# Two transformer blocks on one core: three late sums of squares as pairs of fp32r matmuls, and the last four residuals ahead of the low parts

## The chip, the core and the metric

The kernel runs on one core of one Trainium2 chip. The metric is the device time of one execution in microseconds. The program runs five engines that wait for each other through semaphores: TensorE (matmuls, written PE in the profile), VectorE (DVE), ScalarE (ACT), GpSimd (POOL) and SyncE (SP), which issues the loads of weights.

## The reference

Two blocks run one after the other on 512 positions of width 1024 (the first with 16 meta tokens in front). The first has a sparse attention with chosen keys, a short convolution, a gated mix and a feed forward part; the second has a linear recurrence, two kinds of attention and a feed forward part with a convolution. What matters here are the norms:

```python
def rmsnorm(x, g):
    xf = x.astype(jnp.float32)
    y = xf * lax.rsqrt(jnp.mean(xf * xf, axis=-1, keepdims=True) + EPS)
    return (y * g.astype(jnp.float32)).astype(x.dtype)

# first block, after the mix
h = h + mixed @ w_out[i]
f = rmsnorm(h, norm_ffn_g[i])                      # "ffn"
h = h + (silu(f @ w_gate[i]) * (f @ w_up[i])) @ w_down[i]
out = rmsnorm(h, norm_final_g)                     # folded with the next into "n1"
# second block
h = rmsnorm_2(x, norm1_g[l]); proj = h @ w_in[l]
...
x = x + mixed @ w_out[l]
h2 = rmsnorm_2(x, norm2_g[l])                      # "n2"
u = causal_dwconv(h2 @ w_ff_up[l], conv_ff_w[l], conv_ff_b[l])
...
return rmsnorm_2(x, final_g)                       # "fin2"
```

All inputs and outputs are float32.

## The kernel before

**Layout.** The residual H lies transposed in SBUF, as 8 chunks of 128 channels by 512 positions. Weights come in panels of 1024x128. SyncE loads a panel into RAW (4 slots, a slot is loaded again when its panel has been used), and GpSimd splits it: WH is the value rounded to fp32r (L584), WL the rest (L586), both with SBUF inputs. Operands are split in the same way: ScalarE writes the high part (AH or BH), VectorE the low part (AL or BL). A panel is then 8 chunks of three fp32r matmuls of 512 columns: WH with high, WL with high, WH with low (L645).

**Norms.** The scale 1/rms is applied late, behind the matmuls, since it is the same for all channels of a position. So the panels behind a norm start from the gained but unscaled residual, while the sum of squares is still being made. ScalarE squares each chunk of H, VectorE adds the squares chunk by chunk into SS (128 partitions), and TensorE adds up the partitions in `late_sum` (L714 to L717) and `between_sums` (L908 to L912) by a float32 matmul of `ones` with SS, put between panels that it can do meanwhile. ScalarE takes the root (L1332, L1358), VectorE the reciprocal (L1789, L1841), and the products in PSUM are scaled by it. The norm n1 needs two sums, SS and SSB, since it stands for two norms in a row. The norm fin2 is done in another way and has nothing to do with this change.

**Where the sums stand on TensorE.** For ffn, after 7 of the 8 chunks of two panels. For n1, after the first two panels of stage xa. For n2, after panels 0 and 1 (chunk by chunk in turn, L673 to L675) and half of panel 2 of the stage gv0.

**The end of the second block's output projection.** The stage wo2b has two panels, each holding two chunks of four output rows (`last_rows`, L1044). It writes to four PSUM banks in turn: the first panel gives rows 0 to 3, the second rows 4 to 7, and row 4 + b can start only when VectorE has added row b to H (`last_residual`, L2040 to L2045, which counts up `wo2_free`). Behind each residual ScalarE makes BH and the square (L1491, L1492), and VectorE makes BL (L2051):

```python
for o in range(2):
    last_residual(o)
for o in range(KC):
    dve.wait_ge(b_hi, B_USE["n2"] + o + 1)
    stt(out=BL[:, o], in0=H[:, o], ...)
    for r in ((2, 3, 4), (5,), (6,), (7,))[o] if o < 4 else ():
        last_residual(r)
```

Then come seven additions of squares (L2059), each waiting for the one before, the last of which writes SS. The order of the work on each engine is the order in which the code is written.

Of the kernel before, what the change touches and what calls it, by code (L numbers as in the profile page):

```python
# [15 lines left out]
F32 = mybir.dt.float32  # L16
# [6 lines left out]
P = 128  # L23
# [93 lines left out]
def two_blocks(nc, x, meta_tokens, norm_mix_g, w_in, w_attn_out, conv_w, w_conv_out, w_out, norm_ffn_g, w_gate,  # L117
# [3 lines left out]
    with ExitStack() as ctx:  # L121
        def sem(name):
            return ctx.enter_context(nc.semaphore(name))
# [16 lines left out]
        def again(reg, start):  # L140
            return [start, reg[1]]
# [54 lines left out]
        rq2 = again(r_q, q0)  # L196
        XA = place(rq2, "XA", [P, 4, T + 3])
        YA = place(rq2, "YA", [P, 4, T])
        L = [place(again(r_q, q0), "L0", [P, 2, 2, T]), place(again(r_b, b0 + 4 * 8 * T), "L1", [P, 2, 2, T])]

        rq3 = again(r_q, q0)
# [58 lines left out]
        T2 = place(rt4, "T2", [P, 2, T])  # L260
        rt9 = again(r_t, t0)
        SQB = place(rt9, "SQB", [P, 2, T])
        SSB = place(rt9, "SSB", [P, T])
        SQ8 = place(again(r_t, t0), "SQ8", [P, KC, T])
        SQT = place(rt4, "SQT", [P, 2, T])
        SS = place(rt4, "SS", [P, T])
        ROOT = place(rt4, "ROOT", [P, T])
        rt5 = again(r_t, t0)
# [78 lines left out]
        rstd_ready = {n: sem(f"rstd_ready_{n}") for n in NORMS}  # L347
        LATE = ["ffn", "n1", "n2", "fin2"]
        ss_added = {n: sem(f"ss_added_{n}") for n in LATE}
        ss_summed = {n: sem(f"ss_summed_{n}") for n in LATE}  # L350
        fin_ms = sem("fin_ms")
        gate_scaled, silu_ready, taps_done = sem("gate_scaled"), sem("silu_ready"), sem("taps_done")
# [258 lines left out]
        def _(pe):  # L611
# [101 lines left out]

            def late_sum(name):  # L714

                pe.wait_ge(ss_added[name], KC + 2)
                mm(PX[:, 0, 0:T], ones[:], SS[:], start=True, stop=True).then_inc(ss_summed[name], 1)  # L717

            a_wide = (XH[:, :, 0:N], XL[:, :, 0:N])
            a_x = (XH[:, :, META:N], XL[:, :, META:N])  # L720
# [186 lines left out]

            def between_sums():  # L908

                pe.wait_ge(ss_added["n1"], KC + 2)  # L910
                mm(PX[:, 0, 0:T], ones[:], SS[:], start=True, stop=True)
                mm(PX[:, 1, 0:T], ones[:], SSB[:], start=True, stop=True).then_inc(ss_summed["n1"], 1)  # L912

            stage("xa", b_t, n1, late=1, then=between_sums)
            pe.wait_ge(small_loaded, 16 * (6 + 4))
# [207 lines left out]
        def _(act):  # L1123
# [204 lines left out]
                        go(SQT[:, j], pick(H, c), ACT.Square).then_inc(sq_ready[norm_name], 1)  # L1328

            def root(name):  # L1330
                act.wait_ge(ss_summed[name], 1)
                go(ROOT[:], PX[:, 0, 0:T], ACT.Sqrt, bias=eps_t[:], scale=1.0 / D).then_inc(rt_ready[name], 1)  # L1332

# [13 lines left out]
            with act.Fori(0, KC // 2) as i:  # L1347
                for j in range(2):
                    c = i * 2 + j
                    act.wait_ge(freed["dve"], c + (LETGO["dn2"]["dve"] + 1))  # L1350
                    act.sem_inc(act_seen, 1)
                    go(pick(BH, c), pick(H, c), ACT.Identity, bias=zero_t[:], scale=GF1[:, bass.ds(c, 1)]).then_inc(b_hi, 1)
                    act.wait_ge(ss_added["n1"], c + 1)
                    act.sem_inc(act_seen, 1)
                    go(SQT[:, j], pick(H, c), ACT.Square)
                    go(SQB[:, j], pick(H, c), ACT.Square, scale=VEC[:, 0, bass.ds(c + V_FIN, 1)]).then_inc(sq_ready["n1"], 1)
            act.wait_ge(fin_ms, 1)
            go(ROOT[:], R[:], ACT.Sqrt, bias=eps2_t[:], scale=1.0 / D).then_inc(rt_ready["n1"], 1)  # L1358
            go(RF[:], PX[:, 0, 0:T], ACT.Sqrt, bias=eps_t[:], scale=1.0 / D).then_inc(rt_ready["n1"], 1)
# [164 lines left out]
        def _(dve):  # L1524
# [213 lines left out]
                tt(BL[:, k], QT[:, k], BH[:, k].bitcast(F32), ALU.subtract).then_inc(b_lo, 1)  # L1738
            dve.wait_ge(b_lo, B_USE["y"] + KC)
            nc.vector.memset(WR[:], 0.0).then_inc(wr_cleared, 1)  # L1740
            step(nc.vector.memset(XA[:, :, 0:3], 0.0))


# [31 lines left out]
            def residual(name, scale, to=None):  # L1775
# [3 lines left out]
                with dve.Fori(0, COUNT[name] // 4) as i:  # L1779
                    for j in range(4):  # L1780
# [3 lines left out]
                        if to:  # L1784
                            feed(to[0], i * 4 + j, j % 2, *to[1:])

            def late_scale(name):
                dve.wait_ge(rt_ready[name], 1)
                nc.vector.reciprocal(R[:], ROOT[:]).then_inc(rstd_ready[name], 1)  # L1789
                dve.wait_ge(rstd_ready[name], 1)  # L1790
# [42 lines left out]
                tt(PB6 if c < KC - 1 else SS[:], PB6, SQT[:, c % 2], ALU.add).then_inc(ss_added["n1"], 1)  # L1833


            dve.wait_ge(ss_summed["n1"], 1)
            step(ts(R[:], PX[:, 0, 0:T], EPS, None, ALU.mult))
            settled()
# [181 lines left out]
            step(nc.vector.memset(SBL[:, :, 0:P].bitcast(F32), 0.0))  # L2020
            step(ts(TRI[:, 0], tri[:], 1.0, None, ALU.mult))
            step(ts(TRI[:, 1], nones[:], 1.0, None, ALU.mult))
            for c in range(2):
                sb_mask(2 * c)
                sb_mask(2 * c + 1)
                for i in range(4 * c, 4 * c + 4):
                    rescale(i)
                settled()
                mixed_rows(4 * c)
                mixed_rows(4 * c + 1)  # L2030
                sb_softplus(2 * c)
                sb_softplus(2 * c + 1)
                sb_low(2 * c)
                sb_low(2 * c + 1)
                mixed_rows(4 * c + 2)
                sb_lo(2 * c)
                sb_lo(2 * c + 1)
                mixed_rows(4 * c + 3)
# [5 lines left out]
                    dve.wait_ge(wo2_out, 3 * (o // 4) + o % 4 + 1)  # L2044
                tt(H[:, o], WO2_BANKS[o % 4], H[:, o], ALU.add).then_inc(wo2_free if o < 6 else freed["dve"], 1)  # L2045

            for o in range(2):
                last_residual(o)
            for o in range(KC):
                dve.wait_ge(b_hi, B_USE["n2"] + o + 1)  # L2050
                stt(out=BL[:, o], in0=H[:, o], scalar=VEC[:, 0, V_N2 + o:V_N2 + o + 1], in1=BH[:, o].bitcast(F32),  # L2051
                    op0=ALU.mult, op1=ALU.subtract).then_inc(b_lo, 1)
                for r in ((2, 3, 4), (5,), (6,), (7,))[o] if o < 4 else ():
                    last_residual(r)
            dve.sem_inc(ss_added["n2"], 3)
            for o in range(1, KC):
                dve.wait_ge(sq_ready["n2"], o + 1)
# [81 lines left out]
```

## Time and profile before

| what | value |
|---|---|
| median of 3 runs | 1553.34 us (1552.59 to 1553.67) |
| profiled execution | 1555.63 us |
| its span, first to last instruction | 1553.9 us |
| TensorE busy | 1539.9 us, 99% |
| VectorE, ScalarE, GpSimd busy | 747.5, 395.1, 905.7 us |
| granted TensorE clock, mean | 0.999 of full speed |

The profile is of one execution. "Busy" counts the time in which an engine has an instruction running. The chain of work that ended last is followed back from the last instruction, at each step to what released it. A timeline row has the start in microseconds, the duration, the engine, the line, and what is written from what; in brackets stands how long the engine was idle before it, and what ended that. Matmuls overlap: a row of 0.39 us may stand 0.23 us behind the one before.

### The profile page before, as it was taken

The page shows a single profiled execution, that of the slowest core. Times are in us where ns is not written, and L with a number is a line of the kernel's source. Part 1 is how long each engine was busy: PE and PEld are TensorE (multiplying, and loading weights), DVE is VectorE, ACT ScalarE, POOL GpSimd, SP SyncE. Part 2 cuts the span into 40 slices and gives each one's busy share as a digit, 9 for nine tenths or more (in the row PEclk, how much of TensorE's full clock was granted, in tenths as well). Part 3 has the DMA queues.
Part 4 walks back from the last instruction along what each step waited for, and adds up shares of the span by engine and source line. Part 5 has one row for each costly group of instructions (what it writes and reads, how often), then busy time and mean ns, then how long its engine had stood idle before and what let it go on. Part 6 is the DMA issues. An engine that isn't in the chain of part 4 may idle for free.

```text
span 1553.9 us, 22779 instructions
## 1 busy us (share of the span) xinstructions
PE 1539.9 (99%) x7847; PEld 1291.7 (83%) x7847; DVE 747.5 (48%) x1157; ACT 395.1 (25%) x757; POOL 905.7 (58%) x536
## 2 busy tenths in 40 slices
PE   8999999999999999999999999999999999999998
PEld 7779999988888888888888888777877888888887
DVE  4157840232335354742343245868567751552456
ACT  4221210233442012210010013456564320220122
POOL 5645556544445667766666666653454666666653
PEclk9999999999999999999999999999999999999999
DMA  6223333322223432333333333322222323333322
GB/s 213 82 72 91 85 93 91 86 68 59 64 68 104 147 95 82 108 94 95 100 100 98 95 88 102 93 70 64 60 67 82 94 81 108 96 98 103 95 81 95
DMA packets 266712, 142.67 MB, mean 92 GB/s; under 512 B 6445, under 2 KB 263749, under 8 KB 266389
## 3 DMA queue, kind: packets, MB, share of 16 engines
q1 hardware_dynamic: 265285, 139.16, 30.5%
q10 hardware_dynamic: 1360, 2.56, 0.4%
q8 instruction: 48, 0.79, 0.2%
q14 instruction: 19, 0.16, 0.0%
HBM read 137.38 MB, written 4.19 MB: 91 GB/s over the span
## 4 chain that ended last, share of the span: by engine, by line
PE 95%; DVE 3%; ACT 1%; issue 1%; DMA 0%; ACTq 0%; DVEq 0%
PE PS L645 74%; PE PS L643 12%; PE PS L872 1%; PE PS L849 1%; PE PS L957 1%; PE PS L797 1%; DVE BL L2051 1%; PE PS L875 0%; PE PS L923 0%; PE PS L848 0%; PE PS L862 0%; DVE L L1881 0%; PE PS L1003 0%; DVE L L1864 0%; ACT SBX L1422 0%
## 5 line engine op out<-in xcount | busy, mean ns | idle before, releaser
L586 POOL TENSOR_TENSOR WL<-RAW,WH 128x1024 fp32r<-128x1024 f32 (+1 forms) x259 | 622.7, 2404 | 21.6
L584 POOL TENSOR_SCALAR WH<-RAW 128x1024 fp32r<-128x1024 f32 (+1 forms) x259 | 280.4, 1083 | 607.6 <-DMA RAW<-in_w_in_dram 257.5
L645 PE MATMUL PS<-BH,WH 128*128 128x512 f32 x928 | 366.6, 395 | 1.2 <-DVE BL L2051 1.1
L645 PE MATMUL PS<-BL,WH 128*128 128x512 f32 x928 | 361.4, 389 | 0.0
L645 PE MATMUL PS<-BH,WL 128*128 128x512 f32 x928 | 361.1, 389 | 0.0
L645 PEld LDWEIGHTS PS<-BH,WH 128*128 128x128 f32 x928 | 174.2, 188 | 42.4 <-issue 4.4
L645 PE MATMUL PS<-AH,WH 128*128 128x512 f32 x528 | 205.9, 390 | 0.0
L645 PE MATMUL PS<-AL,WH 128*128 128x512 f32 x528 | 205.4, 389 | 0.0
L645 PE MATMUL PS<-AH,WL 128*128 128x512 f32 x528 | 205.4, 389 | 0.0
L645 PEld LDWEIGHTS PS<-BH,WL 128*128 128x128 f32 x928 | 174.3, 188 | 37.2 <-issue 1.7
L645 PEld LDWEIGHTS PS<-BL,WH 128*128 128x128 f32 x928 | 174.2, 188 | 36.6
L645 PE MATMUL PS<-XH,WH 128*128 128x512 f32 x288 | 119.9, 416 | 0.0
L645 PEld LDWEIGHTS PS<-AH,WH 128*128 128x128 f32 x528 | 99.1, 188 | 21.2 <-issue 1.0
L645 PEld LDWEIGHTS PS<-AL,WH 128*128 128x128 f32 x528 | 99.1, 188 | 20.6
L645 PEld LDWEIGHTS PS<-AH,WL 128*128 128x128 f32 x528 | 99.1, 188 | 20.3
L645 PE MATMUL PS<-XH,WL 128*128 128x512 f32 x288 | 112.3, 390 | 0.0
L645 PE MATMUL PS<-XL,WH 128*128 128x512 f32 x288 | 112.3, 390 | 0.0
L643 PE MATMUL PS<-XH,WH 128*128 128x264 f32 (+2 forms) x528 | 107.3, 284 | 0.4 <-DVE XL L1583 0.4
L643 PE MATMUL PS<-XH,WL 128*128 128x264 f32 (+2 forms) x528 | 106.5, 283 | 0.0
L643 PE MATMUL PS<-XL,WH 128*128 128x264 f32 (+2 forms) x528 | 106.5, 283 | 0.0
L1783 DVE SCALAR_TENSOR_TENSOR H<-PS,H 128x512 f32 x40 | 27.6, 691 | 141.5 <-PE PS L645 141.5
L643 PEld LDWEIGHTS PS<-XH,WH 128*128 128x128 f32 (+1 forms) x528 | 81.3, 187 | 1.9 <-DVE XL L1583 0.7
(334 smaller groups left out, 1817.4 us busy)
## 6 DMA issues: line engine op xcount, KB each, us to landing
RAW<-in_w_in_dram SPq DMA_DIRECT2D x89, 512.0 KB, 3.4
RAW<-in_w_ff_up_dram SPq DMA_DIRECT2D x44, 512.0 KB, 3.6
RAW<-in_w_gate_dram SPq DMA_DIRECT2D x22, 512.0 KB, 3.6
RAW<-in_w_up_dram SPq DMA_DIRECT2D x22, 512.0 KB, 3.6
RAW<-in_w_down_dram SPq DMA_DIRECT2D x16, 512.0 KB, 3.6
RAW<-in_w_ff_down_dram SPq DMA_DIRECT2D x16, 512.0 KB, 3.6
RAW<-in_w_out_dram SPq DMA_DIRECT2D x10, 512.0 KB, 3.7
RAW<-in_w_conv_out_dram SPq DMA_DIRECT2D x8, 512.0 KB, 3.7
```

What stands on the lines that cost most here:

```text
L584: nc.gpsimd.tensor_scalar(WH[:, slot, 0:kc], RAW[:, slot, 0:kc], 1.0, 1.0, ALU.mult, ALU.mult).then_inc(w_hi, 1)
L586: nc.gpsimd.tensor_tensor(WL[:, slot, 0:kc], RAW[:, slot, 0:kc], WH[:, slot, 0:kc].bitcast(F32), ALU.subtract).then_inc(w_ready, 1)
L643: last = mm(into[0:rows, h, 0:wide], w[:, w_at, k, 0:rows], a[:, k, h * wide:(h + 1) * wide], start=st, stop=sp_)
L645: last = mm(bank_of(name, i)[0:rows], w[:, w_at, k, 0:rows], a[:, k, :], start=st, stop=sp_)
L797: last = mm(dst[:, 0:min(EXT[b], BANK)], lhs, KI[r:r + 64, 0:min(EXT[b], BANK)], start=True, stop=True)
L849: mm(PX[:, 0, 0:min(large_e, BANK)], QS[:, 1], head[:, 0:min(large_e, BANK)], start=True, stop=True).then_inc(qk_done, 1)
L872: mm(PB7[:, 0 if t <= few else P:2 * P], V[:, t, at], PT[:, 0 if t <= few else 1:2, t * P:(t + 1) * P], start=t == 0, stop=False, skip_gro ...
L957: last = mm(SB_SET[n % 2][:, to - max(SBW[j], 2 * P):to], TRI[:, 0 if j == i else 1], spaced(part, n % 2, j), start=False, stop=True, skip ...
L1783: stt(out=h, in0=bank_of(name, j), scalar=scale, in1=h, op0=ALU.mult, op1=ALU.add).then_inc(freed["dve"], 1)
L2051: stt(out=BL[:, o], in0=H[:, o], scalar=VEC[:, 0, V_N2 + o:V_N2 + o + 1], in1=BH[:, o].bitcast(F32), op0=ALU.mult, op1=ALU.subtract).then_ ...
```

## The change

SS is split like any other operand: ScalarE copies it to SSH, rounded to fp32r, and VectorE subtracts, which gives SSL (in the place of SS). TensorE adds the partitions of both into one PSUM bank with two fp32r matmuls, with ONE, an fp32r copy of `ones`. The same is done with SSB. ONE lies where other tiles come later, so it is written twice. The norm fin2 keeps its matmuls. On VectorE the last residuals are put in another order: four before the first low part, and one behind each of the next four low parts.

```diff
+        rq4 = again(r_q, q0 + 8448)
+        SSH = place(rq4, "SSH", [P, T], F32R)
+        SSBH = place(rq4, "SSBH", [P, T], F32R)
+        ONE = place(rq4, "ONE", [P, P], F32R)
...
+        SSBL = place(again(rt9, rt9[0]), "SSBL", [P, T], F32R)
         SSB = place(rt9, "SSB", [P, T])
...
+        SSL = place(again(rt4, rt4[0]), "SSL", [P, T], F32R)
         SS = place(rt4, "SS", [P, T])
...
+        SUM_USE = {"ffn": 0, "n1": 1, "n2": 3}
...
             def late_sum(name):
-                pe.wait_ge(ss_added[name], KC + 2)
-                mm(PX[:, 0, 0:T], ones[:], SS[:], start=True, stop=True).then_inc(ss_summed[name], 1)
+                pe.wait_ge(one_ready, 2 if name == "n2" else 1)
+                pe.wait_ge(ss_lo, SUM_USE[name] + 1)
+                mm(PX[:, 0, 0:T], ONE[:], SSH[:], start=True, stop=False)
+                mm(PX[:, 0, 0:T], ONE[:], SSL[:], start=False, stop=True).then_inc(ss_summed[name], 1)
...
             def between_sums():
-                pe.wait_ge(ss_added["n1"], KC + 2)
-                mm(PX[:, 0, 0:T], ones[:], SS[:], start=True, stop=True)
-                mm(PX[:, 1, 0:T], ones[:], SSB[:], start=True, stop=True).then_inc(ss_summed["n1"], 1)
+                pe.wait_ge(ss_lo, SUM_USE["n1"] + 2)
+                for n, (own, after_b) in enumerate(((SSH, SSBH), (SSL, SSBL))):
+                    mm(PX[:, 0, 0:T], ONE[:], own[:], start=n == 0, stop=n == 1)
+                    last = mm(PX[:, 1, 0:T], ONE[:], after_b[:], start=n == 0, stop=n == 1)
+                last.then_inc(ss_summed["n1"], 1)
...
             def root(name):
+                act.wait_ge(ss_added[name], KC + 2)
+                go(SSH[:], SS[:], ACT.Copy).then_inc(ss_hi, 1)
                 act.wait_ge(ss_summed[name], 1)
...
+            act.wait_ge(ss_added["n1"], KC + 2)
+            go(SSH[:], SS[:], ACT.Copy).then_inc(ss_hi, 1)
+            go(SSBH[:], SSB[:], ACT.Copy).then_inc(ss_hi, 1)
             act.wait_ge(fin_ms, 1)
...
             nc.vector.memset(WR[:], 0.0).then_inc(wr_cleared, 1)
+            ts(ONE[:], ones[:], 1.0, None, ALU.mult).then_inc(one_ready, 1)
...
+            def sum_low(name, whole, hi, lo, n=1):
+                dve.wait_ge(ss_hi, SUM_USE[name] + n)
+                tt(lo[:], whole[:], hi[:].bitcast(F32), ALU.subtract).then_inc(ss_lo, 1)
+
             def late_scale(name):
+                sum_low(name, SS, SSH, SSL)
                 dve.wait_ge(rt_ready[name], 1)
...
+            sum_low("n1", SS, SSH, SSL)
+            sum_low("n1", SSB, SSBH, SSBL, 2)
             dve.wait_ge(ss_summed["n1"], 1)
...
             step(ts(TRI[:, 1], nones[:], 1.0, None, ALU.mult))
+            ts(ONE[:], ones[:], 1.0, None, ALU.mult).then_inc(one_ready, 1)
...
-            for o in range(2):
+            for o in range(4):
                 last_residual(o)
...
-                for r in ((2, 3, 4), (5,), (6,), (7,))[o] if o < 4 else ():
-                    last_residual(r)
+                if o < 4:
+                    last_residual(o + 4)
```

How it moves the work. On VectorE, from the last residuals to the reciprocal of n2, before (H from PSUM is a residual, BL a low part, SQ the squares):

```order
L2045 TENSOR_TENSOR H<-PS,H 128x512 [waits wo2_out] x2
L2051 SCALAR_TENSOR_TENSOR BL<-H,VEC,BH 128x512 [waits b_hi]
L2045 TENSOR_TENSOR H<-PS,H 128x512 [waits wo2_out]
L2045 TENSOR_TENSOR H<-PS,H 128x512 [waits panel_done]
L2045 TENSOR_TENSOR H<-PS,H 128x512 [waits wo2_out]
L2051 SCALAR_TENSOR_TENSOR BL<-H,VEC,BH 128x512 [waits b_hi]
L2045 TENSOR_TENSOR H<-PS,H 128x512 [waits wo2_out]
```

and now, at the same place and, behind the "...", at the end of the sum:

```order
L2071 TENSOR_TENSOR H<-PS,H 128x512 [waits wo2_out] x3
L2071 TENSOR_TENSOR H<-PS,H 128x512 [waits panel_done]
L2077 SCALAR_TENSOR_TENSOR BL<-H,VEC,BH 128x512 [waits b_hi]
L2071 TENSOR_TENSOR H<-PS,H 128x512 [waits wo2_out]
...
L2085 TENSOR_TENSOR SS<-PS,SQ_128 128x512 [waits ss_added_n2,sq_ready_n2]
L1807 TENSOR_TENSOR SSL<-SS,SSH 128x512 [waits ss_hi]
L1812 RECIPROCAL R<-ROOT 128x512 [waits rt_ready_n2]
```

Residuals 2 and 3 have moved ahead of the first low part, and a subtraction stands between the last addition and the reciprocal.

On TensorE, the sums of n1 between the panels of stage xa, before:

```order
L645 MATMUL PS<-BL,WH 128x512 [waits b_lo]
L911 MATMUL PS<-SS,ones 128x512 [waits ss_added_n1]
L912 MATMUL PS<-SSB,ones 128x512
L645 MATMUL PS<-BH,WH 128x512 [waits b_lo,freed_dve,w_ready]
L645 MATMUL PS<-BH,WL 128x512
```

and now:

```order
L653 MATMUL PS<-BL,WH 128x512 [waits b_lo]
L922 MATMUL PS<-SSH,ONE 128x512 [waits ss_lo]
L923 MATMUL PS<-SSBH,ONE 128x512
L922 MATMUL PS<-SSL,ONE 128x512
L923 MATMUL PS<-SSBL,ONE 128x512
L653 MATMUL PS<-BH,WH 128x512 [waits b_lo,freed_dve,w_ready]
```

Two matmuls have become four, and they wait for the low parts of the sums where they waited for the sums.

## Rows read from the trace of the kernel before

**Rows 1.** The page: busy time of the engines, and the chain by engine.

```profile
PE 1539.9 (99%) x7847; PEld 1291.7 (83%) x7847; DVE 747.5 (48%) x1157; ACT 395.1 (25%) x757; POOL 905.7 (58%) x536
...
PE 95%; DVE 3%; ACT 1%; issue 1%; DMA 0%; ACTq 0%; DVEq 0%
```

**Rows 2.** Chain of waits, around the sum of ffn (start us, us, what).

```profile
599.94 20.40 PE PS L645 x90
620.34 0.86 PE PS L717 x2
```

**Rows 3.** Timeline at the sum of ffn, VectorE and GpSimd (start us, us, engine).

```profile
613.63 0.69 DVE L1773 TENSOR_TENSOR SS<-SS,SQT 128x512 f32<-128x512 f32 x1
614.66 1.04 POOL L584 TENSOR_SCALAR WH<-RAW 128x1024 fp32r<-128x1024 f32 x1 [1.95 <-DMA RAW<-in_w_up_dram]
```

**Rows 4.** Timeline at the sums of n1, VectorE and TensorE.

```profile
979.38 0.68 DVE L1833 TENSOR_TENSOR SS<-PS,SQT 128x512 f32<-128x512 f32 x1
981.51 0.39 PE L645 MATMUL PS<-BL,WH 128*128 128x512 f32 x1
983.69 0.40 PE L645 MATMUL PS<-BH,WL 128*128 128x512 f32 x1
```

**Rows 5.** Timelines: a ScalarE copy, a TensorE restart, GpSimd after n1's sums.

```profile
630.85 0.63 ACT L1345 ACTIVATE AH<-T 128x512 f32 x1 [3.80 <-DVE T L1812]
...
974.80 0.50 PE L645 MATMUL PS<-BH,WH 128*128 128x512 f32 x1
...
985.19 1.05 POOL L584 TENSOR_SCALAR WH<-RAW 128x1024 fp32r<-128x1024 f32 x1 [6.92 <-DMA RAW<-in_w_in_dram]
```

**Rows 6.** Timeline of VectorE from the last residuals to SS of n2.

```profile
1173.03 1.37 DVE L2045 TENSOR_TENSOR H<-PS,H 128x512 f32<-128x512 f32 x2 [2.25 <-PE PS L1049]
1174.61 2.97 DVE L2051 SCALAR_TENSOR_TENSOR BL<-H,VEC,BH 128x512 fp32r<-128x512 f32 x1 [0.21 <-ACT BH L1491]
...
1179.30 1.39 DVE L2051 SCALAR_TENSOR_TENSOR BL<-H,VEC,BH 128x512 fp32r<-128x512 f32 x1
...
1184.04 0.73 DVE L2051 SCALAR_TENSOR_TENSOR BL<-H,VEC,BH 128x512 fp32r<-128x512 f32 x1
...
1185.30 5.51 DVE L2051 SCALAR_TENSOR_TENSOR BL<-H,VEC,BH 128x512 fp32r<-128x512 f32 x4
1190.73 4.71 DVE L2059 TENSOR_TENSOR PS<-PS,SQ 128x512 f32<-128x512 f32 x6
1195.54 0.69 DVE L2059 TENSOR_TENSOR SS<-PS,SQ 128x512 f32<-128x512 f32 x1
```

**Rows 7.** Timeline of GpSimd in the same stretch.

```profile
1174.63 2.40 POOL L586 TENSOR_TENSOR WL<-RAW,WH 128x1024 fp32r<-128x1024 f32 x1
...
1180.23 2.73 POOL L586 TENSOR_TENSOR WL<-RAW,WH 128x1024 fp32r<-128x1024 f32 x1
1185.10 1.06 POOL L584 TENSOR_SCALAR WH<-RAW 128x1024 fp32r<-128x1024 f32 x1 [2.14 <-DMA RAW<-in_w_ff_up_dram]
1186.24 2.69 POOL L586 TENSOR_TENSOR WL<-RAW,WH 128x1024 fp32r<-128x1024 f32 x1
1197.43 1.05 POOL L584 TENSOR_SCALAR WH<-RAW 128x1024 fp32r<-128x1024 f32 x1 [8.49 <-DMA RAW<-in_w_ff_up_dram]
```

**Rows 8.** Timeline of TensorE in the same stretch.

```profile
1174.64 0.39 PE L1049 MATMUL PS<-AH,WL 128*128 128x512 f32 x1
...
1177.36 0.39 PE L1049 MATMUL PS<-AH,WL 128*128 128x512 f32 x1
1178.24 0.50 PE L1049 MATMUL PS<-AH,WH 128*128 128x512 f32 x1 [0.49 <-DVE H L2045]
...
1180.87 0.39 PE L1049 MATMUL PS<-AH,WL 128*128 128x512 f32 x1
...
1192.85 0.39 PE L645 MATMUL PS<-BL,WH 128*128 128x512 f32 x1
...
1197.56 0.39 PE L645 MATMUL PS<-BH,WL 128*128 128x512 f32 x1
```

## What was predicted

> **What bounds the kernel now.** I read the page first: TensorE is busy for 99% of the span, and the chain of work that ended last is 95% TensorE [rows 1]. So time comes off only where TensorE itself does less or waits less; work on another engine counts only where TensorE stands still for it. Then I read the chain of waits around the first late sum, to get two prices. Ninety panel matmuls take 20.40 us there, 0.227 us each, and the f32 matmul over the ones, two records, takes 0.86 us [rows 2]. Last I read the timelines of VectorE, GpSimd and TensorE around each of the three sums [rows 3 to 8]. The reader is to see there when the sum of squares is ready, when TensorE asks for it, and where VectorE is held up behind GpSimd.
>
> **Four f32 matmuls become eight fp32r ones.** The norms ffn and n2 have one sum each, n1 has two: four f32 matmuls at 0.86 us, 3.44 us of TensorE [rows 2]. Each becomes two matmuls of panel kind, 2 x 0.227 = 0.45 us. Saved are 0.41 us each, 1.64 us in all, if nothing waits. As bounds: an fp32r matmul with new operands cannot be below the panel pitch, and if it cost as much as an f32 record (0.43 us) the saving would be nothing. I take the panel pitch, since element kinds and shape are those of a panel matmul. The Trainium skill (FP8 and Floating Point Precision, TensorE Precision Notes) says that true FP32 makes four passes. Four passes at this trace's pitch would be 0.91 us and the saving 1.8 us instead of 1.64; no trace of a pass is visible here, only the two records, so the measured 0.86 stands in the sum.
>
> **What is put in front of each sum.** Before, TensorE needed only SS. Now ScalarE copies SS to SSH (0.63 us, by its copy to AH [rows 5]), VectorE subtracts (0.69 us uncontended, by its addition to SS, also all in SBUF [rows 3]), with some 0.03 us for each hand-over: about 1.4 us from SS to the matmul. ScalarE now loads its square root table behind the copy; there are more than 3 us until the root is wanted at each norm, so that is hidden.
>
> *ffn.* SS is ready at 613.63 + 0.69 = 614.32 [rows 3]. SSH follows at 615.0. The subtraction then meets GpSimd's operation that ends at 615.70 [rows 3] and ends at 616.3. TensorE asks at about 620.2 (the chain row: 599.94 + 20.40 [rows 2]). Slack 3.9 us, so the saving is whole: **-0.41 us**.
>
> *n1.* SS is ready at 979.38 + 0.68 = 980.06 [rows 4]. SSH at 980.72, SSBH half a microsecond later, SSL at 981.43, SSBL at 982.04 (subtractions 0.61 us apart). GpSimd does nothing until 985.19 [rows 5], so none of it is held up. TensorE would ask at 981.51 + 0.23 = 981.74 [rows 4]. It therefore waits to 982.10 and pays 0.11 us at the restart (a first matmul after a wait shows 0.50 us, not 0.39 [rows 5]). Then four matmuls: the second panel matmul behind the sum starts at 982.10 + 0.11 + 5 x 0.227 = 983.35, where it started at 983.69 before [rows 4]. Net **-0.34 us** of the possible 0.82. Behind the waiting matmul on TensorE stand only panels 2 and 3 of xa, which nobody needs early.
>
> *The small copies into ONE* (128x128, twice) stand on VectorE at the start of co and after TRI. I cost them at nothing: in both places VectorE runs on into a wait for TensorE. If that cover were gone, each would be about 0.2 us.
>
> **The reordered residuals (n2).** This is where both edits meet. Before, VectorE does residuals 0 and 1, then the first low part BL, which starts at 1174.61 and lasts 2.97 us [rows 6] because GpSimd's subtraction runs to 1174.63 + 2.40 = 1177.03 [rows 7]; it ends 0.55 us after that. Residual 2 comes behind it, so TensorE, which needs that bank, starts at 1178.24 instead of 1177.36 + 0.23 = 1177.59 [rows 8]: 0.65 us plus 0.11 for the restart, 0.76 us. From 1177.36 to the matmul at 1197.56 [rows 8] there are 12 + 60 + 2 = 74 matmuls and the sum, 74 x 0.227 + 0.86 = 17.64 us; it took 20.20. So 2.56 us were lost: 0.76 for this bank, the rest for low parts that came late.
>
> Now residuals 2 and 3 go ahead. The panel that residual 3 needs ends at 1174.64 + 0.39 = 1175.03 [rows 8], so residual 3 ends at 1175.76. BL 0 starts at 1175.7, inside the same GpSimd operation, and ends at 1177.58 as before: the two residuals are hidden in time that was blocked. The 0.76 us goes. From there every low part comes one place earlier. BL 1 ends at 1178.83. BL 2 ends at 1180.69, where BL 1 ended (1179.30 + 1.39 [rows 6]). BL 3 is held until GpSimd's subtraction is over (1180.23 + 2.73 [rows 7]) and ends at 1183.51, and BL 4 takes the free slot of 0.73 us at 1184.04 [rows 6], to 1184.77. GpSimd's next piece hangs on the last panel of wo2b. That ended at 1180.87 + 0.39 and the piece began 3.84 us later at 1185.10 [rows 7, 8]; now it ends at 1180.47, so the piece begins near 1184.31, in the middle of BL 4, and gets the port behind it. BL 5 then ends near 1186.2, BL 6 is held by the 2.7 us subtraction [rows 7] to 1189.0, BL 7 ends at 1189.65. Before, it ended at 1190.81 (1185.30 + 5.51 [rows 6]).
>
> TensorE starts the gate panels at 1177.59 + 12 x 0.227 = 1180.31 and needs BL k at 1180.31 + 1.36 k. All are in time but BL 6 (1188.47 wanted, 1189.0 there): 0.57 + 0.11 = 0.68 us lost. It would reach the sum at 1180.31 + 60 x 0.227 + 0.68 = 1194.6.
>
> But the sum is not ready. From the end of BL 7 to the end of SS were 1195.54 + 0.69 - 1190.81 = 5.42 us [rows 6], seven dependent additions, unchanged. SS is ready at 1195.07, SSH at 1195.74, and SSL is asked for at 1195.77. At that moment GpSimd is due again: it began 1197.43 - (1192.85 + 0.39) = 4.19 us after the first gate panel ended [rows 7, 8], and that panel now ends near 1191.35. So its conversion (1.05 us) begins near 1195.54 and ends at 1196.59, just ahead of SSL, which has both inputs in SBUF like BL. SSL ends 0.55 us later, at 1197.14. TensorE starts the sum at 1197.18 and the second panel matmul behind it at 1197.18 + 0.11 + 3 x 0.227 = 1197.97, where it started at 1197.56 [rows 8]. Net **+0.41 us**: the stalls of 2.5 us that the new order removes come back as a wait of 2.6 us at the sum.
>
> The Trainium skill (SBUF — State Buffer, SBUF: two separate sides) says that the shared pair of ports goes to whichever of the two engines starts first. Here the row of BL 0 starts 0.02 us ahead of GpSimd's and was held all the same, so the starts in the trace don't settle such close races. For SSL, 0.23 us behind, rule and rows give the same 1197.14; asked for just ahead, the rule gives 1196.5 and the row 1197.14.
>
> **Sum.** -0.41 - 0.34 + 0.41 = -0.34 us. The profiled execution took 1555.63 us, 1.7 us more than its span of 1553.9; it would be 1555.3. The median of the runs shown is 1553.34, 2.3 us less, so I forecast **1553.0 us**, no change. A measurement of this kernel can tell about 0.2%, 3.1 us: faster is below 1550.2, slower above 1556.5.
>
> **Rivals.** *A: SSL gets the port ahead of GpSimd.* If GpSimd is due 0.3 us later or SS is ready 0.3 us earlier, SSL ends at 1196.45, the matmul at 1197.56 is at 1197.3 and n2 gives -0.3: in all -1.0 us, 1552.3. For it: the two are 0.23 us apart and the arrivals of weights in [rows 7, 8] differ by 0.35 us (3.84 and 4.19). Against it: both must shift the right way.
>
> *B, slower: SSL misses the gap between GpSimd's two operations.* If SSL is asked for after 1196.59, the 2.4 us subtraction is under way; SSL ends near 1199.6, TensorE starts 2.5 us later than in the forecast, and the total is -0.34 + 2.5 = +2.1, 1555.5. It decides from 0.8 us more delay on the VectorE chain, or an equal advance of GpSimd. For it: one more held low part is enough. Against: 0.8 us is more than the spread of the arrivals. Were a second low part also held for a whole subtraction, 2 us more, it would pass 1556.5.
>
> *C, faster: the sum keeps up.* If the low parts come free of GpSimd and SSL is there when TensorE asks, the whole is -1.64 - 2.56 = -4.2 us, 1549.1. Against it: seven additions and the new 1.4 us are in series behind BL 7, and TensorE has only 16 matmuls, 3.6 us, between its first use of BL 7 and the sum, where that chain takes 5.4 + 1.4 us.
>
> *D: the fp32r pair is no cheaper than f32* (0.43 us a matmul): -0.34 + 8 x 0.2 = +1.3, 1554.6. Nothing in the rows speaks for it.
>
> **Chances.** Forecast 0.55, A 0.22, B 0.13, C 0.05, D 0.05. Faster by over 0.2% is C, 0.05. Slower by over 0.2% is the worst third of B, 0.04. Within: 0.91. The range runs from A less the spread of the runs shown (0.7 us), 1551.6, to B, 1555.5.
>
> **What would show it.** ffn: the sum's matmuls at the panel pitch, no wait. n1: a wait of 0.3 to 0.5 us for SSBL. n2: no wait of TensorE for residual 2; BL 0 still ending near 1177.6; BL 7 about 1.2 us earlier; the sum waiting for SSL by 2 to 3 us, and SSL longer than 0.69 us. I am wrong if TensorE does not wait at the third sum, or if SSL ends after 1198 on this clock.

## The result, and the profile after

| | before | changed |
|---|---|---|
| median, taken in turns on one chip | 1553.16 us of 15 runs (1552.20 to 1553.68) | 1556.99 us of 15 runs (1555.41 to 1557.93) |
| ratio of the times | | 1.0024 (95%: 1.0016 to 1.0031) |
| profiled execution | 1555.63 us | 1556.89 us |
| its span | 1553.9 us | 1555.2 us |

The change costs 3.8 us. The forecast was 1553.0 us with a range to 1555.5. (Of all executions below, one of the changed kernel with GpSimd gated ran in a slower state, 1701.70 us at a granted clock of 0.851; the ratios leave it out.) By the sums' own matmuls there is less to do, and yet the time is longer. The page of the changed kernel, busy time by engine and the chain by engine:

```profile
PE 1538.4 (99%) x7847; PEld 1292.1 (83%) x7847; DVE 755.9 (49%) x1163; ACT 397.5 (26%) x761; POOL 907.8 (58%) x536
...
PE 92%; DVE 4%; ACT 2%; issue 1%; DMA 0%; ACTq 0%; DVEq 0%
```

TensorE is busy 1.5 us less than in [rows 1], and its share of the chain has fallen from 95% to 92%: VectorE and ScalarE have taken its place. The timelines say where. First TensorE at the sums of ffn and n1 (start us, us, engine, line, tiles, in brackets the idle time before and what ended it):

```profile
620.48 0.39 PE L726 MATMUL PS<-SSH,ONE 128*128 128x512 f32 x1
620.71 0.40 PE L727 MATMUL PS<-SSL,ONE 128*128 128x512 f32 x1
...
981.64 0.39 PE L653 MATMUL PS<-BL,WH 128*128 128x512 f32 x1
982.23 0.50 PE L922 MATMUL PS<-SSH,ONE 128*128 128x512 f32 x1 [0.21 <-DVE SSBL L1807]
...
983.49 0.40 PE L653 MATMUL PS<-BH,WL 128*128 128x512 f32 x1
```

At ffn the pair runs at the panel pitch, 0.23 us from one to the next, with no wait. At n1 there is a short wait for SSBL. From the start of the last panel matmul ahead of the sums to the start of the second one behind them are 983.49 - 981.64 = 1.85 us, against 983.69 - 981.51 = 2.18 in [rows 4]. These two are as forecast. Now the third sum. VectorE and, behind the last "...", GpSimd, from the last residuals on:

```profile
1172.91 2.73 DVE L2071 TENSOR_TENSOR H<-PS,H 128x512 f32<-128x512 f32 x4 [2.28 <-PE PS L1061]
1175.56 2.02 DVE L2077 SCALAR_TENSOR_TENSOR BL<-H,VEC,BH 128x512 fp32r<-128x512 f32 x1
...
1179.37 1.07 DVE L2077 SCALAR_TENSOR_TENSOR BL<-H,VEC,BH 128x512 fp32r<-128x512 f32 x1
...
1180.96 2.29 DVE L2077 SCALAR_TENSOR_TENSOR BL<-H,VEC,BH 128x512 fp32r<-128x512 f32 x1
...
1183.78 5.66 DVE L2077 SCALAR_TENSOR_TENSOR BL<-H,VEC,BH 128x512 fp32r<-128x512 f32 x4
...
1194.17 0.69 DVE L2085 TENSOR_TENSOR SS<-PS,SQ 128x512 f32<-128x512 f32 x1
1195.55 0.69 DVE L1807 TENSOR_TENSOR SSL<-SS,SSH 128x512 fp32r<-128x512 f32 x1 [0.70 <-ACT SSH L1344]
...
1174.62 2.41 POOL L594 TENSOR_TENSOR WL<-RAW,WH 128x1024 fp32r<-128x1024 f32 x1
1178.84 1.06 POOL L592 TENSOR_SCALAR WH<-RAW 128x1024 fp32r<-128x1024 f32 x1 [1.81 <-DMA RAW<-in_w_ff_up_dram]
1179.98 2.72 POOL L594 TENSOR_TENSOR WL<-RAW,WH 128x1024 fp32r<-128x1024 f32 x1
```

BL 0 is held by GpSimd's subtraction, BL 2 gets in between GpSimd's two operations, and BL 3 is held by the second subtraction. All of this was worked out ahead, and it stands within 0.3 us of the forecast's times. TensorE behind it:

```profile
1193.56 0.39 PE L653 MATMUL PS<-BL,WH 128*128 128x512 f32 x1
1196.39 0.47 PE L726 MATMUL PS<-SSH,ONE 128*128 128x512 f32 x1 [2.44 <-DVE SSL L1807]
1196.70 0.40 PE L727 MATMUL PS<-SSL,ONE 128*128 128x512 f32 x1
...
1197.71 0.63 PE L653 MATMUL PS<-BH,WH 128*128 128x512 f32 x1
1198.14 0.63 PE L653 MATMUL PS<-BH,WL 128*128 128x512 f32 x1
...
1201.05 0.39 PE L653 MATMUL PS<-BL,WH 128*128 128x512 f32 x1
1201.28 0.39 PE L653 MATMUL PS<-BH,WH 128*128 128x512 f32 x1
```

The wait of 2.44 us was forecast (2.6). What follows wasn't: from 1197.7 to 1201 the matmuls stand 0.43 us apart, not 0.23. Three stretches of 4 us show it as the granted clock (after the ends and the length of each: busy time and number of instructions of PE, PEld, DVE, ACT and POOL, then the clock):

```profile
1193.00:1197.00 4.00, 1.56 (x8) 0.99 (x7) 2.34 (x4) 1.91 (x2) 2.26 (x2) 1.00 0.67 201
1197.00:1201.00 4.00, 4.00 (x12) 3.11 (x11) 3.14 (x1) 2.18 (x3) 3.92 (x3) 0.57 0.02 4
1201.00:1205.00 4.00, 4.00 (x19) 3.28 (x19) 2.27 (x4) 0.78 (x1) 0.97 (x1) 1.00 0.44 131
```

The clock falls about 1.3 us after the wait is over. It is then at its lower level, 1.2 GHz: its mean is 0.57 in the middle stretch, and 0.51 from 1197.70 to 1201.05. In the middle stretch 12 matmuls run where 19 run in the one behind it. Eight of them stand 0.20 us further apart each: about 1.6 us. The Trainium skill (TensorE: Matmul & The Clock Gate, HAM oscillation) says that idle gaps set the matmul array back to the half clock. The trace agrees in kind, but the gaps that the page warns of are longer than the 2.44 us that came before this fall; here the measurement decides.

### The profile page after: what moved, and what is told of

It reads as the page before. It is cut to its first block, busy times and chain, and to the rows that moved or that the text cites. A ratio compares the mean times of both kernels' runs of the same rounds, so it can differ in the third digit from the quotient of the medians.

```text
span 1555.2 us, 22791 instructions
## 1 busy us (share of the span) xinstructions
PE 1538.4 (99%) x7847; PEld 1292.1 (83%) x7847; DVE 755.9 (49%) x1163; ACT 397.5 (26%) x761; POOL 907.8 (58%) x536
## 3 DMA queue, kind: packets, MB, share of 16 engines
q10 hardware_dynamic: 1360, 2.56, 0.4%
## 4 chain that ended last, share of the span: by engine, by line
PE 92%; DVE 4%; ACT 2%; issue 1%; DMA 0%; ACTq 0%; DVEq 0%
PE PS L653 71%; PE PS L651 12%; PE PS L882 1%; PE PS L859 1%; PE PS L969 1%; DVE BL L2077 1%; PE PS L807 1%; PE PS L885 0%; PE PS L935 0%; PE PS L858 0%; DVE L L1906 0%; PE PS L872 0%; PE PS L1015 0%; DVE H L2071 0%; DVE L L1889 0%
```

## The experiments

Each was timed in five rounds in turns with the kernel before, whose medians were 1553.34 to 1553.38 us (33 to 35 runs). In the table "reach" is the time from the start of the first of the last residuals on VectorE to the start of the addition that writes SS. It was 22.51 in the traced execution of before (1195.54 - 1173.03, [rows 6]), and 21.26 after. The waits are those of the one traced execution. A difference of 1.3 to 1.7 us between medians stands at the edge of these intervals, so for each such difference the trace has to show the place where it arises.

| kernel | median us | ratio (95%) | reach | waits of TensorE at n2 |
|---|---|---|---|---|
| before, once more | 1553.57 | 1.0001 (0.9992 to 1.0010) | 18.22 | none |
| new order alone | 1554.68 | 1.0008 (0.9999 to 1.0017) | 21.40 | BL 0.5, SS 0.3 |
| split sums alone | 1551.81 | 0.9991 (0.9982 to 1.0000) | 18.21 | none |
| changed, third sum later | 1553.20 | 0.9998 (0.9989 to 1.0007) | 21.38 | BL 0.4 |
| changed, TensorE kept busy | 1555.81 | 1.0014 (1.0005 to 1.0022) | 21.41 | BL 0.5, then filled |
| before + 0.9 us ahead of BL 0 | 1554.95 | 1.0010 (1.0002 to 1.0019) | 21.64 | BL 0.35, SS 0.7 |
| before + 0.9 us behind BL 0 | 1555.03 | 1.0008 (0.9999 to 1.0017) | 21.84 | BL 0.55, SS 0.7 |
| changed, n2's sum in f32 | 1554.38 | 1.0006 (0.9997 to 1.0014) | 21.49 | BL 0.55, SS 0.35 |
| changed, GpSimd gated | 1552.47 | 0.9994 (0.9985 to 1.0002) | 16.44 | none |
| new order alone, GpSimd gated | 1553.53 | 1.0002 (0.9993 to 1.0011) | 16.40 | none |
| split alone, n1's sums later | 1551.74 | 0.9992 (0.9983 to 1.0000) | 18.25 | none |
| the same, GpSimd gated | 1551.68 | 0.9990 (0.9981 to 0.9999) | 15.66 | none |

**The kernel before, once more** (no edit).

> The kernel before, unchanged, once more, as a second trace of it: the changed kernel's trace is 1.3 us longer than the one trace of before, but its median is 3.8 us above before's. Theory A (the trace of before happens to be a long execution): time 1553.2, and a trace whose span is nearer 1551.5 than 1553.9, with the 2.4 us less in one place. Rival (the missing 2.5 us are a cost of the changed kernel that its own trace does not show): span again 1553.9.

The new trace took 1553.74 us, close to its median, where the one that the prediction was made from took 1555.63. VectorE in it, and GpSimd's first piece behind the last "...":

```profile
1175.18 0.77 DVE L2051 SCALAR_TENSOR_TENSOR BL<-H,VEC,BH 128x512 fp32r<-128x512 f32 x1 [0.20 <-ACT BH L1491]
...
1180.56 0.93 DVE L2051 SCALAR_TENSOR_TENSOR BL<-H,VEC,BH 128x512 fp32r<-128x512 f32 x1
...
1182.02 5.07 DVE L2051 SCALAR_TENSOR_TENSOR BL<-H,VEC,BH 128x512 fp32r<-128x512 f32 x4
...
1191.82 0.69 DVE L2059 TENSOR_TENSOR SS<-PS,SQ 128x512 f32<-128x512 f32 x1
...
1174.35 1.06 POOL L584 TENSOR_SCALAR WH<-RAW 128x1024 fp32r<-128x1024 f32 x1 [7.80 <-DMA RAW<-in_w_ff_up_dram]
1175.50 2.73 POOL L586 TENSOR_TENSOR WL<-RAW,WH 128x1024 fp32r<-128x1024 f32 x1
```

BL 0 takes 0.77 us, not the 2.97 of [rows 6]. Here it is asked for while GpSimd still converts (until 1175.41), waits, and gets the gap ahead of the subtraction. In [rows 6, 7] it was asked for at 1174.61, 0.06 us after the conversion before that subtraction had ended, and was held for all of it:

```profile
1173.50 1.05 POOL L584 TENSOR_SCALAR WH<-RAW 128x1024 fp32r<-128x1024 f32 x1 [7.55 <-DMA RAW<-in_w_ff_up_dram]
```

The waits of TensorE that followed there, the 2.56 us which the prediction counted, don't exist here: the same 74 matmuls and the sum take 17.63 us (1195.57 - 1177.94), as the prediction has them without a stall. Of the 35 runs of before that were taken beside the kernels with the clearing, 31 took 1552.05 to 1554.05 us and four 1555.82 to 1556.35, with the same granted clock; of the 94 others on record none took more than 1554.21. So an execution like the traced one is the seldom one. (That those four had a held BL 0 too is likely, not shown.)

**The new order alone.**

```diff
-            for o in range(2):
+            for o in range(4):
                 last_residual(o)
...
-                for r in ((2, 3, 4), (5,), (6,), (7,))[o] if o < 4 else ():
-                    last_residual(r)
+                if o < 4:
+                    last_residual(o + 4)
```

> Only the new order of the residuals; all sums stay float32. Theory A (what costs is the wait of 2.4 us at the third sum and the half clock for 3.4 us behind it): without the copy and the subtraction the sum is ready near 1194.9, TensorE waits 1.0 us instead of 2.4, the clock stays whole, as after the waits of 1.1 us in the kernel before; 2.5 us of stalls saved, 1.1 given back: -1.4 us, 1551.8. Rival B (the new order itself costs, through where it meets GpSimd): 1553.2 or more.

Theory A wanted a gain, and the order costs: +1.3 us. The interval just takes in no change, but the trace has the place: set matmul by matmul beside the second trace of before, it loses 0.76 us at the wait for BL and 0.57 at the wait for SS, restarts included, and nothing behind them. It shows the low parts of the changed kernel, and SS later by 3.2 us of reach:

```profile
1181.11 2.30 DVE L2051 SCALAR_TENSOR_TENSOR BL<-H,VEC,BH 128x512 fp32r<-128x512 f32 x1
...
1194.31 0.69 DVE L2059 TENSOR_TENSOR SS<-PS,SQ 128x512 f32<-128x512 f32 x1
```

**The split sums alone** (the changed kernel with the diff above undone).

> Only the sums as pairs of fp32r matmuls; the residuals stay in the old order. Theory A: the sum of n2 is ready at 1196.2 + 1.4 = 1197.6, or near 1199 if the subtraction falls behind GpSimd's conversion that starts at 1197.4; TensorE, which asks at 1196.5, waits 1.1 to 2.5 us: n2 +0.7 to +2.1, with -0.75 from ffn and n1: 0.0 to +1.4, 1553.2 to 1554.6, and 1.7 us more where the clock falls. Rival B (the split is harmless, the new order costs): -0.8 to 0, 1552.4 to 1553.2.

Theory A was wrong here too: it took SS from the long execution of before. The result is -1.57 us, beside -1.16 by the terms of the forecast without n2's wait (0.41 + 0.34 + 0.41). SSL is in time, with nothing between the panel matmul and the pair:

```profile
1191.95 0.69 DVE L1807 TENSOR_TENSOR SSL<-SS,SSH 128x512 fp32r<-128x512 f32 x1 [0.70 <-ACT SSH L1344]
...
1193.23 0.39 PE L726 MATMUL PS<-SSH,ONE 128*128 128x512 f32 x1
```

So the sums alone give -1.57 and the order alone +1.30. Added up that would be -0.3; together they took +3.8. The 4.1 us between are what neither of them has alone: SS is late by the order and 1.4 us more go by before SSL, so that TensorE waits for 2.44 us and the clock falls.

**The third sum behind all of panel 2**, 12 matmuls later.

```diff
-                    panel(name, 2, 2, rhs, ready, kc=kc, ks=halves(kc)[0])
+                    panel(name, 2, 2, rhs, ready, kc=kc)
                     sums()
-                    panel(name, 2, 2, rhs, ready, kc=kc, ks=halves(kc)[1])
```

> The changed kernel with its third sum behind the whole of panel 2 instead of behind its first half: 12 more matmuls, 2.7 us, before TensorE asks for it. Theory A: wait (2.4 us) and fall of the clock (1.7 us) go, all else stays: 1557.0 - 4.1 = 1552.9 or less, span 1551. If the scale of the norm is then late for panel 4, up to 1 us comes back. Rival B (order or port contention costs elsewhere): at most the 2.4 us of the wait, 1554.6.

3.8 us less than the changed kernel: the wait (2.44) and the low clock (1.6) make 4.0. The sum's first matmul starts at 1197.14 with no wait, and the granted clock is 1.00 from 1189 to 1205.

**TensorE kept busy during the wait**, by ten matmuls into the sum's bank, which the sum then overwrites.

```diff
+                if name == "n2":
+                    for _ in range(10):
+                        mm(PX[:, 0, 0:T], WH[:, (FIRST["gv0"] + 2) % SLOTS, 0, :], BH[:, 0, :], start=True, stop=True)
                 pe.wait_ge(one_ready, 2 if name == "n2" else 1)
```

> The changed kernel with ten more fp32r matmuls (128x512, their result overwritten by the sum) in front of the wait for the third sum: 2.27 us of matmuls where TensorE stood idle for 2.44 us. Clock theory: the sum still starts when SSL is ready (1196.3), but the granted clock stays at 1.0 and the 3.4 us at 0.5 go: -1.6 us, 1555.4. Rival (the fall is not tied to this wait): 1557 or more.

1.2 us less than the changed kernel, though the sum starts 0.5 us later (1196.93), since SSL was ready later. The clock stays whole:

```profile
1194.41 2.43 PE L726 MATMUL PS<-BH,WH 128*128 128x512 f32 x10
1196.93 0.47 PE L729 MATMUL PS<-SSH,ONE 128*128 128x512 f32 x1
```

```profile
1197.00:1201.00 4.00, 4.00 (x18) 3.28 (x19) 2.62 (x1) 2.17 (x3) 3.92 (x3) 1.00 0.01 4
```

So the fall of the clock is worth about 1.6 us, 1.2 net and the 0.5 of the later sum, and its cause is TensorE's idle time, not the late SSL as such.

**0.9 us of VectorE work ahead of BL 0, or behind it**, in the kernel before: a clearing of WR, which nobody needs there.

```diff
             for o in range(2):
                 last_residual(o)
+            step(nc.vector.memset(WR[:], 0.0))
```

> The kernel before, old order and float32 sums, with one clearing of WR (128x1024, no longer needed there; 0.91 us in the trace) on VectorE between residual 1 and the first low part. Gap theory: in the usual execution of before the first low part is asked for while GpSimd converts (1174.35 to 1175.41 in the second trace), gets the port between conversion and subtraction (1175.50), and lasts 0.77 us; in the first trace it was asked for 0.06 us after the conversion's end and lasted 2.97 us, and that cost 1.9 us at the end. Asked for 0.7 us later, every execution misses the gap: first low part near 2.9 us, time 1555.0 to 1555.5 with a narrow spread. Rival (the first trace was slow for another reason): the clearing costs VectorE 0.7 us and TensorE, waiting for residual 2, at most as much: 1553.4 to 1554.1.

```diff
                 stt(out=BL[:, o], in0=H[:, o], ...)
+                if o == 0:
+                    step(nc.vector.memset(WR[:], 0.0))
```

> The same clearing of WR in the kernel before, but between the first low part and residual 2: the same VectorE work behind the gap. Gap theory: the low part still gets the gap (0.77 us); residual 2 comes 0.8 us later, inside the time in which GpSimd holds the port anyway: 1553.4 to 1554.0. Rival (it is the work, not the gap): the same time as with the clearing ahead of the low part.

My theory was then that all is decided by whether BL 0 gets the gap before GpSimd's first subtraction. It fell: both cost 1.6 to 1.7 us (for the second the interval just takes in no change; its trace has two waits of TensorE, 0.55 and 0.70 us). In the second kernel BL 0 does get the gap, and SS is as late. In the first BL 0 wasn't held at all, and GpSimd's subtraction took 3.38 us. First the rows of this kernel, then, behind the "...", those of the second:

```profile
1174.13 0.91 DVE L2049 MEMSET WR<- 128x1024 f32 x1 [0.16 <-issue]
1174.96 0.63 DVE L2052 SCALAR_TENSOR_TENSOR BL<-H,VEC,BH 128x512 fp32r<-128x512 f32 x1
...
1174.48 3.38 POOL L586 TENSOR_TENSOR WL<-RAW,WH 128x1024 fp32r<-128x1024 f32 x1
...
1175.14 0.75 DVE L2051 SCALAR_TENSOR_TENSOR BL<-H,VEC,BH 128x512 fp32r<-128x512 f32 x1 [0.20 <-ACT BH L1491]
1176.05 0.91 DVE L2054 MEMSET WR<- 128x1024 f32 x1 [0.16 <-issue]
...
1175.30 2.86 POOL L586 TENSOR_TENSOR WL<-RAW,WH 128x1024 fp32r<-128x1024 f32 x1
```

The clearing isn't held by a subtraction that is under way: in the second kernel it starts 0.75 us into one and takes the same 0.91 us. So it isn't shown that the clearing itself kept GpSimd back in the first. It may have been BL 0, which stood ready behind the clearing when GpSimd's conversion ended.

What the two kernels and the new order share is the second subtraction. In the kernel before, the low part that gets the gap ahead of it is BL 3 (the row of 0.93 us above). In these three kernels, where VectorE is 0.9 us or more behind at this point, BL 2 has that gap, and BL 3 is held throughout (2.29 us after, 2.30 with the order alone). Put together from the traces, with the first residual as zero: BL 1 starts at 5.20 after and at 4.07 before, with as many residuals ahead of it (BL 0 held, +1.13); BL 3 ends at 10.34 and 7.89 (+2.45, of which 1.32 from missing the second gap); BL 4 to 7 take 5.66 and 5.07 us (+0.6). That is the 3.0 us of reach.

**The changed kernel with n2's sum as before**, one f32 product, without the copy and the subtraction ahead of it (the cut shows TensorE's part).

```diff
+                if name == "n2":
+                    pe.wait_ge(ss_added[name], KC + 2)
+                    mm(PX[:, 0, 0:T], ones[:], SS[:], start=True, stop=True).then_inc(ss_summed[name], 1)
+                    return
```

> The changed kernel with n2's sum left as the float32 product (the sums of ffn and n1 split, the new order). Theory A (the terms add: order +1.2, ffn and n1 -0.75, wait of 2.4 us and clock fall only with the split sum at n2): 1553.9, a wait of 0.3 at the sum, clock whole. Rival B (the loss is the order's alone, whatever n2's sum is): 1556 or more.

1554.38 us. Theory A holds within the interval: the edits add up as long as TensorE's wait is short, and splitting n2's sum in this order costs 2.6 us, where without the new order it pays.

**GpSimd gated**: it starts on the weights of gv0's third panel only when all eight low parts are written. One line, in three kernels: the changed one, the new order alone, and the best one below.

```diff
+            pool.wait_ge(b_lo, B_USE["n2"] + KC)
             splits(FIRST["gv0"] + 2, FIRST["ed2"], twice=2)
```

> The changed kernel, with GpSimd made to wait for all eight low parts of n2 before it begins to split the weights of gv0's third panel. Theory A (the low parts are late because GpSimd's two-input operations hold them): low parts 1 to 7 unheld at about 0.75 us each, the last done near 1184, SS at about 1189.5 instead of 1194.17, SSL at about 1191, no wait of TensorE at the third sum, clock whole there; 1551.8 us, as with only the split sums. Rival B (the order itself costs, or the split weights then come late for gv0's panel): 1554 or more, with a wait of TensorE for GpSimd's weights or for SSL.

> Only the new order (residuals ahead of low parts, float32 sums), with the same wait of GpSimd for all eight low parts. Theory A: the hold goes, SS near 1189.5, no wait of TensorE at n2; about 1553.3, 1.4 below the same order without the gate (1554.68). Rival B: the order itself costs: 1554.7 as without it.

Both come near theory A (0.7 and 0.2 us above it): 4.5 us less than the changed kernel, 1.15 less than the same order ungated. VectorE and GpSimd of the first:

```profile
1175.50 2.03 DVE L2078 SCALAR_TENSOR_TENSOR BL<-H,VEC,BH 128x512 fp32r<-128x512 f32 x1
...
1180.58 0.73 DVE L2078 SCALAR_TENSOR_TENSOR BL<-H,VEC,BH 128x512 fp32r<-128x512 f32 x1
...
1181.84 2.73 DVE L2078 SCALAR_TENSOR_TENSOR BL<-H,VEC,BH 128x512 fp32r<-128x512 f32 x4
...
1189.30 0.69 DVE L2086 TENSOR_TENSOR SS<-PS,SQ 128x512 f32<-128x512 f32 x1
1190.69 1.82 DVE L1808 TENSOR_TENSOR SSL<-SS,SSH 128x512 fp32r<-128x512 f32 x1 [0.70 <-ACT SSH L1345]
...
1184.92 1.05 POOL L592 TENSOR_SCALAR WH<-RAW 128x1024 fp32r<-128x1024 f32 x1 [7.94 <-DVE BL L2078]
```

BL 1 to 7 take 0.73 us or less each, SS is 4.8 us of reach earlier, and though SSL is now the one held (1.82 us), it is there when TensorE asks. Set matmul by matmul beside the second trace of before, the new order alone with the gate loses nothing from 1176 us to the end, where it lost 1.33 us without. So without GpSimd's operations in between the order costs nothing at this place: its price comes through them. The weights are delayed by some 6 us, and nobody waits for them. (The kernel before with the gate alone wasn't run; it had no wait at n2 to lose.) The Trainium skill (SBUF — State Buffer, Who interferes with whom) says that this pair of ports is the only thing on which the two engines contend, as an exclusive lock; the low parts with and without the gate agree.

**n1's sums in the middle of a panel**, and that with the gate: the old order, all three sums split.

```diff
-                    if then:
-                        then()
...
+                        if then and p == 2:
+                            panel(name, p, p, rhs, ready, kc=kc, ks=halves(kc)[0], **kw)
+                            then()
+                            panel(name, p, p, rhs, ready, kc=kc, ks=halves(kc)[1], **kw)
```

> Old order of residuals, all sums split, and the sums of n1 moved 12 matmuls (2.7 us) down, into the middle of panel 2 of stage xa. In the run with only the sums split TensorE waits 0.36 us there and restarts at 0.11. Theory: both go, -0.45 us against 1551.8: 1551.3. Rival: the scale of n1 comes 2.2 us later, and a stage behind it on VectorE (XC) is late for TensorE: 1552 or more.

> Old order, all three sums split, n1's sums in the middle of the panel, and GpSimd's wait for the eight low parts. Theory A (the old order's hold is small in undisturbed executions, 0.8 us over 8 low parts): 1551.5, as without the gate, with less spread from run to run. Rival B: the weights of gv0's third panel, needed near 1191, come late: 1552.5 to 1554 with a wait of TensorE for GpSimd there.

The wait at n1 goes, but the median stays: 1551.74 against 1551.81 without the edit (one of its 12 executions took 1558.43 us, the others at most 1552.16). In the trace the half microsecond is lost again 80 us later, at 1065, where TensorE waits 0.61 us for a tile L. The second trace of before has a wait of 0.55 us there too, the trace of the split sums alone has none, and the same kernel with the gate, which differs only behind this place, has 0.8 us less there. So this place varies from execution to execution, and whether the edit has anything to do with it is open. The gate adds nothing either (1551.68), since the old order had no wait to lose, though SS is 2.6 us earlier. This is the fastest of all, 1.7 us below before, with the interval just clear of 1. The split sums in the old order have nearly all of it.

## Why the prediction was wrong

**Right: the matmuls.** From the last panel matmul ahead of the sum to the second one behind it, ffn takes 0.91 us, against 1.32 in both traces of before: -0.41 as forecast. At n1 these are 1.85 and 2.17 us, -0.32 where -0.34 was forecast; in five more traces with n1's sums at this place the gain is 0.03 to 0.36, by how long TensorE waits for SSBL. Rival D (the pair no cheaper) is out.

**Right in effect, not in size: the square root table.** The forecast gave its load more than 3 us behind the copy at each norm. At n2 the copy to SSH ended at 1195.52 and the sum was there 1.6 us later; the load takes 1.28 us and was only just hidden.

**Right: the path of the low parts in the new order.** BL 0 ended at 1177.6, BL 1 at 1178.84, BL 3 at 1183.25 (forecast 1183.51), BL 7 at 1189.44 (1189.65), SS at 1194.86 (1195.07). BL 6 was in time, which the forecast denied by 0.5 us; in four other traces of this order without the gate TensorE did wait 0.44 to 0.55 us for it. In the changed kernel this shifts nothing, since TensorE waits for SSL afterwards. SSL was ready at 1196.24, not 1197.14: GpSimd was due at 1194.66, 0.9 us ahead of the estimate, and SSL got the gap behind its conversion. That is the forecast's own way for SSL, only earlier, and not rival A, in which SSL goes ahead of the conversion. It put the sum's first matmul at 1196.39, 0.8 us ahead of the forecast, and so lessened the loss.

**Wrong: "the stalls of 2.5 us that the new order removes come back as a wait of 2.6 us at the sum".** The second half is right (2.44 measured). The first isn't true of most executions: the kernel before has no such stalls in them. The forecast took the sum's difference, -0.34 us, from an execution that was 2.3 us above its median, and applied it to that median. Its own sentence gives the distance, 2.3 us, and leaves it unexplained; it was nearly the size of the stalls at the place of the edit. Aligned matmul by matmul, the long trace of before is 0.6 us ahead of the other up to 1177 us and 2.0 behind it at the end. Nearly all of these 2.6 us arise at three places: 0.8 us at the matmul that waited for residual 2, 0.3 at 1186.75, and 1.4 at the one that waited for BL at 1189.54. Against the undisturbed trace the order removes nothing, it puts SS back by 3 us of reach: the 2.56 us that the forecast credited are the larger part of the miss of 4.2 us.

**Missing: the clock.** No step of the forecast asked what TensorE does after an idle stretch longer than those in the trace of before (0.49 us, and this one, after both of which the clock stayed whole). It cost 1.6 us more. The two terms, 2.56 and 1.6, come to the whole miss of 4.2 us, and that they fit so well is in part luck: SSL came 0.8 us early, a gain that is lost in the spread between executions. TensorE in the trace of before that was read for the prediction:

```profile
1189.54 0.50 PE L645 MATMUL PS<-BH,WH 128*128 128x512 f32 x1 [1.13 <-DVE BL L2051]
```

**The sum as measured**, matmul by matmul from the undisturbed trace of before (1553.74) to that of after (1556.89): up to the third sum -0.7 us, at the third sum's first matmul +1.9, behind the pair +1.6, at the end of the low clock and to the end of the program +3.2. Single places vary by up to 0.8 us from trace to trace, so the total rests on the medians, +3.8. The 0.7 us between the two are the places of these executions: this one of before was 0.6 us above the median of the 15, that of after 0.1 below its own.

**Rival B** had the right sign and nearly the right price (1555.5), by another way: SSL didn't miss its gap. Its remark that "one more held low part is enough" is what had happened, one step earlier, in the comparison with most executions of before.

## What to carry to other kernels

Compare the profiled execution's time with the median before using its stalls: where it is above by about the size of the stalls next to the edit, they may be of this execution alone, and the base of the sum must be one without them. Where VectorE and GpSimd share a port, the price of a delay on VectorE need not be its length, but whether the next operation still falls in the gap between two GpSimd operations: 0.9 us of work put SS back by 3.4 us and the end by 1.6. Gating GpSimd's work, when its result isn't wanted soon, takes this dependence away: it gave 4.5 us where the low parts were late and cost nothing where they weren't. An edit that puts work in front of a consumer has to be costed together with any other that makes the same chain late: here the one alone gained 1.6 us, the other alone cost 1.3, and together they cost 3.8. And a wait of TensorE like the 2.44 us here is to be costed with the clock behind it.

## What the runs showed of the hardware

- An operation of VectorE that waits while GpSimd converts gets the port ahead of GpSimd's next operation and ends 0.53 to 0.54 us after the conversion (BL 0 before, once more: 1175.95 against 1175.41; SSL after: 1196.24 against 1195.71); the subtraction then shows 2.71 to 2.73 us instead of 2.40. Asked for 0.06 us after the conversion's end, it was held through all of the subtraction (2.97 us).
- A clearing of 128x1024 f32 on VectorE, with no input from SBUF, took the same 0.91 us beside a subtraction of GpSimd that was under way. Where a low part stood ready behind such a clearing, GpSimd's subtraction took 3.38 us; which of the two kept it back isn't shown.
- After an idle stretch of 2.44 us, which ended at 1196.39, TensorE's clock was at 1.2 GHz from 1197.7 to 1201 (mean 0.51), and then whole again. With the stretch filled by other matmuls it didn't fall (1.00), nor after idle stretches of 0.49 and 1.13 us.
